# Order of a few decode and output steps in a hybrid attention kernel on one core

## The chip, the cores and the metric

The program runs on one core of a Trainium2 chip. The metric is the device time of one execution in microseconds, and lower is better. All data is fp32 unless a row of the profile says otherwise.

## What is computed

One layer of a model with two kinds of attention, for a prompt of 512 tokens and for 8 decode sequences of one new token each that have 4096 cached tokens. Cut to what matters here:

```python
xn = rmsnorm(x, norm_pre)
(qa, kvc, kvs, kvw, gn, ga, qd, kvd, krp, gb, ma, mb) = split(xn @ w_in)
# branch a (NSA): compressed, selected (top 16 blocks of 64) and window attention, gated and added
o_a = g0 * attend(q, compressed) + g1 * attend(q_rot, selected) + g2 * attend(q_rot, window)
# branch b (MLA): scores over latent pages and their rope rows, softmax, weighted sum of the pages
s = (q_lat @ c.T + q_pe @ kr.T) * MLA_SCALE
o_b = (softmax(s) @ c) @ w_kv_up_v
# merge
pa = (o_a * silu(ga)) @ w_proj_a
pb = (o_b * silu(gb)) @ w_proj_b
h = sigmoid(ma) * pa + sigmoid(mb) * pb
y = x + rmsnorm(h @ w_out, norm_post)
```

It also returns the new cache rows and the shifted window buffer.

## The kernel before

Each engine has its own instruction stream, written out by hand in one function, `build`. Semaphores alone join the streams: `pe.wait_ge(S["dp"], n)` holds TensorE until that semaphore has reached n. The time falls into a projection phase (to about 180 us), the *step loop* (to 456 us), the tail of gates and projections (to 612 us) and the output product with its norm (to the end).

**The step loop** has steps d = 0 to 50. In each step up to 48, the prompt part takes two *units* (a head and a tile of 128 queries). TensorE computes their scores (`scores(d)`, recorded at L1254) for step d, the transposes of the probabilities of step d-1 (`transposes`, L1264), and the output product of step d-2 (`outputs`, L1280). VectorE takes the maxima (L2341), ScalarE the exponentials (L1862), and each copies one of the two transposed units (VectorE L2349, ScalarE by the copy helper L1654). `scores(d)` waits for the exponentials of step d-1.

**Decode work** is dealt out over the same steps by dictionaries that are built by hand. There are 16 *latent pairs* p2 = 0 to 15. Pair p2 reads pages m = 2\*p2 and m = 2\*p2+1 (`latent_scores`, L1362), and with its second page 128 rows of rotary keys, the *rope rows* (L1366). There are also window and selected chunks, whose 512 keys are first transposed (`dec_keys`, L1327, with copies to SBUF by ScalarE and one by VectorE), then scored (`dec_scores`, L1337). `SOFT_at[d]` names the chunk whose softmax falls in step d: latent pairs at 16, 20, 24, 28, 32, 36, 40, 42, 44, 46, 48, others at 17, 22, 25, 26, 29, 30, 33, 34, 37, 38. `K_at` holds the steps with key transposes: 16, 21, 24, 28, 32, 36. `G_at` puts 16 half gates (`gate_half`, L1393, 16 matmuls each) in steps 23 to 49, among them number 14 in step 48 and number 15 in step 49.

The softmax of a chunk goes: scores in bank 5, maximum on VectorE (L2395), exponential on ScalarE into `Pd` (L1879, semaphore `dp`), the *turn* `dec_transposes` on TensorE (L1408), a copy on ScalarE (`dt_copied`; into `PTd` for window and selected chunks), and in the next step the product with the pages (`latent_outputs`, L1377) or the values (`dec_outputs`, L1346), which VectorE folds in (`dec_fold`, L2423 and L2425). The turn stands in one of two places of TensorE's stream: at the end of step d, in bank 7, for the steps in `TURN_FIRST` (17, 20, 22, 25, 26, 29, 30, 33, 34, 37, 38, 40, 42, 44, 46, 48), and otherwise (16, 24, 28, 32, 36) behind `scores(d+1)` in bank 6. The keys use banks 6, 4, 7 and 6 for their four parts, so the turn of a key step waits in bank 6 for ScalarE's copy of the fourth part.

```python
if d - 1 in SOFT_at and d - 1 not in TURN_FIRST:
    dec_transposes(d - 1)
...
if d in TURN_FIRST:
    dec_transposes(d)
```

**Loads.** SyncE issues page loads of 8 x 256 KB each (`latents(m)`, L688), in program order, each behind a wait for its slot. Pages 26 (job `J_LATE`) lie in `W`, over operands of the prompt scores that must be done with. ScalarE issues the rope rows (`load_rope`, L1809), 256 KB a pair, into one buffer, `KRR`: pair p2+1 once the scores of pair p2 are done, and `latent_scores` waits for them ahead of the pair's second page.

**Last rows.** The final product comes in column halves (`out_product`, L1605). VectorE adds each part (`rows_added`, L2739), ScalarE squares it (L1959) and takes the root, VectorE works out the inverse root (`root_of`, L2774 to L2782), and writes y (`out_half`, L2795). For four halves GpSimd multiplies the row by `norm_post` ahead of that; for the last one, (3, 0), it does so in two parts of 256 columns (L875). SyncE stores y.

Of the kernel before, what the change touches and what calls it, by code (L numbers as in the profile page):

```python
# [16 lines left out]
P = 128  # L17
# [146 lines left out]
def build(nc, t):  # L164

    ctx = ExitStack()
    with ctx:
# [157 lines left out]
        for r in range(4):  # L325
# [8 lines left out]
                 J_LATE: [W[:, at:at + 512] for at in (0, 512, 1024, 2048, 8256, 8768, 9280, 9792)]}  # L334
        HALF_PAGES = (cst[:, 1283:1539], OF[:, 1792:2048])

# [80 lines left out]
        TURN_FIRST = {d for d in SOFT_at if d >= 16 and d not in K_at}  # L417
# [200 lines left out]
        def turn_bank(c):  # L618

            return bank[7 if SOFT_STEP[c["q"]] in TURN_FIRST else 6]  # L620

# [4 lines left out]
        def _(sp):  # L626
# [151 lines left out]
            sp.dma_start(t["o_win"][:, 0:WINDOW - 1, :], t["win"][:, 1:WINDOW, :]).then_inc(S["win_moved"], 16)  # L778
# [19 lines left out]
            sp.wait_ge(S["y_out"], 160)  # L798
            sp.wait_ge(S["stored"], QUERIES_MOVED)
            sp.wait_ge(S["win_moved"], 16)  # L800
# [3 lines left out]
        def _(pool):  # L804
# [66 lines left out]
            for part, added in enumerate((out_added["c21a", 1], out_added["c21", 1])):  # L871
                lo = part * 256
                pool.wait_ge(S["z_by_dve"], added)
                pool.wait_ge(S["inv_root"], ROWS_DONE.index(1) + 3)
                pool.tensor_tensor(normed[:, 1536 + lo:1792 + lo], H[:, 3 * D_MODEL + lo:3 * D_MODEL + lo + 256],  # L875
                                   OB[:, lo:lo + 256], ALU.mult).then_inc(S["normed"], 1)

# [54 lines left out]
        def _(pe):  # L932
# [417 lines left out]
            def latent_scores(m):  # L1350
                b, i2, p2 = m // 4, m % 2, m // 2
                if i2 == 1:
                    pe.wait_ge(S["kr_landed"], 16 * (p2 + 1))
                elif mla[p2]["q"]:
                    pe.wait_ge(S["dp"], mla[p2]["q"])
# [8 lines left out]
                if i2 == 1:  # L1364
                    for j in range(4):
                        mm = pe.matmul(bank[5][32 * j:32 * j + 32, 0:P], QRd[:, b * 32:(b + 1) * 32], KRR[:, j * P:(j + 1) * P],  # L1366
# [30 lines left out]
            def dec_transposes(d):  # L1397
# [19 lines left out]
            for d in range(1, PAIRS + 2):  # L1417
# [19 lines left out]
                if d in G_at:  # L1437
# [204 lines left out]
        def _(act):  # L1642
# [1296 lines left out]
```

## Time and profile before

| | us |
|---|---|
| median of 3 runs | 675.36 |
| fastest, slowest of them | 674.79, 683.52 |
| the profiled execution | 675.11 |
| its span on the core | 673.3 |

The rows shown below are of one profiled execution. A timeline row gives start, duration, engine, line, operation, what is written from what is read, the count of merged instructions, and in brackets the idle time of the engine before it with what ended that time. Times are in us from the span's start. "issue" means that the profile shows nothing that the engine waited for.

### The profile page before, as it was taken

The page shows a single profiled execution, that of the slowest core. Times are in us where ns is not written, and L with a number is a line of the kernel's source. Part 1 is how long each engine was busy: PE and PEld are TensorE (multiplying, and loading weights), DVE is VectorE, ACT ScalarE, POOL GpSimd, SP SyncE. Part 2 cuts the span into 40 slices and gives each one's busy share as a digit, 9 for nine tenths or more (in the row PEclk, how much of TensorE's full clock was granted, in tenths as well). Part 3 has the DMA queues.
Part 4 walks back from the last instruction along what each step waited for, and adds up shares of the span by engine and source line. Part 5 has one row for each costly group of instructions (what it writes and reads, how often), then busy time and mean ns, then how long its engine had stood idle before and what let it go on. Part 6 is the DMA issues. An engine that isn't in the chain of part 4 may idle for free.

```text
span 673.3 us, 15352 instructions
## 1 busy us (share of the span) xinstructions
PE 651.5 (97%) x5771; PEld 433.0 (64%) x5771; DVE 447.4 (66%) x1232; ACT 214.8 (32%) x586; POOL 79.5 (12%) x91
## 2 busy tenths in 40 slices
PE   9999999999999998899999998999999999999994
PEld 3444444553576765667777675678788888886442
DVE  2198899686577777766665663637585757649864
ACT  0311321776444454444443532421011111110221
POOL 0344343125000000120211000000000000000011
PEclk9999999999999999999999999999999999999997
DMA  8999999999989999978759789975411111027011
GB/s 337 417 422 424 424 427 400 361 369 283 344 296 378 398 395 413 374 245 316 273 179 361 230 276 403 407 280 219 157 63 63 63 63 63 1 109 300 2 63 62
DMA packets 67587, 179.44 MB, mean 267 GB/s; under 512 B 7513, under 2 KB 16498, under 8 KB 60218
## 3 DMA queue, kind: packets, MB, share of 16 engines
q1 hardware_dynamic: 56088, 125.14, 50.9%
q0 software_dynamic: 8640, 48.90, 17.9%
q10 hardware_dynamic: 2786, 4.42, 1.8%
q8 instruction: 46, 0.75, 0.4%
q14 instruction: 27, 0.22, 0.1%
HBM read 169.38 MB, written 12.72 MB: 270 GB/s over the span
## 4 chain that ended last, share of the span: by engine, by line
PE 88%; DVE 5%; issue 2%; ACT 2%; SPq 1%; DMA 1%; DVEq 0%; another core or an unknown queue 0%; ACTq 0%
PE bank L1554 20%; PE bank L973 12%; PE bank L1393 8%; PE bank L1605 7%; PE bank L1254 5%; PE bank L958 4%; PE bank L1377 4%; PE bank L1362 3%; PE bank L1280 3%; PE bank L1264 3%; PE bank L1583 2%; PE bank L1137 2%; PE bank L1327 2%; PE bank L1337 1%; PE bank L1408 1%
## 5 line engine op out<-in xcount | busy, mean ns | idle before, releaser
L973 PE MATMUL bank<-W,XG 128*128 128x494 f32 x192 | 83.5, 579 | 0.0
L1862 ACT ACTIVATE projP<-bank,projP 128x128 f32<-128x128 f32 (+3 forms) x96 | 49.8, 523 | 41.8 <-DVE projP L2341 41.5
L2641 DVE TENSOR_TENSOR projP<-projP,bank 128x260 f32<-128x260 f32 x81 | 32.6, 423 | 42.3 <-PE bank L1554 41.6
L1654 ACT ACTIVATE projP<-bank 128x128 f32<-128x128 f32 (+5 forms) x87 | 33.7, 391 | 84.0 <-PE bank L1554 47.7
L1393 PE MATMUL bank<-W 128*128 128x260 f32 x256 | 60.4, 389 | 0.0
L973 PEld LDWEIGHTS bank<-W,XG 128*128 128x128 f32 x192 | 35.2, 192 | 35.6 <-issue 35.0
L1393 PEld LDWEIGHTS bank<-W 128*128 128x128 f32 x256 | 47.3, 190 | 10.8 <-issue 3.7
L2341 DVE CUSTOM_DVE_ANT_0 bank<-bank,maskb 128x128 f32<-128x128 f32 (+3 forms) x96 | 45.8, 511 | 12.0 <-PE bank L1254 10.6
L1654 ACT ACTIVATE W<-bank 128x512 f32<-128x512 f32 (+2 forms) x69 | 40.1, 582 | 38.7 <-PE bank L1016 11.6
L809 POOL DMA_INDIRECT ring<-cmp,idxi x32 | 38.6, 1207 | 67.5 <-DVE VV L2052 47.7
L1254 PE MATMUL bank<-W 64*128 64x128 f32 (+7 forms) x192 | 46.0, 466 | 0.5 <-ACT projP L1862 0.4
L2052 DVE TENSOR_TENSOR VV<-ring 128x1024 f32<-128x1024 f32 x32 | 39.2, 1223 | 7.4 <-DMA ring<-cmp,idxi 5.1
L869 POOL TENSOR_TENSOR ring<-XG,OB 128x512 f32<-128x512 f32 x3 | 3.8, 1264 | 303.5 <-DVE XG L2739 303.5
L1554 PE MATMUL bank<-ring 128*128 128x260 f32 x168 | 38.2, 383 | 0.0
L1264 PE MATMUL bank<-cst,projP 128*128 128x128 f32 x240 | 36.7, 280 | 0.3
L1554 PEld LDWEIGHTS bank<-ring 128*128 128x128 f32 x168 | 31.8, 190 | 5.3 <-issue 0.4
L1554 PE MATMUL bank<-W 128*128 128x260 f32 x144 | 34.6, 383 | 0.0
L1939 ACT ACTIVATE projP<-projP 128x260 f32<-128x260 f32 x28 | 11.3, 420 | 71.0 <-DVE projP L2641 70.9
L1264 PEld LDWEIGHTS bank<-cst,projP 128*128 128x128 f32 x240 | 26.8, 140 | 9.6 <-issue 5.3
L1986 DVE TENSOR_SCALAR projP<-projP,sm 128x128 f32<-128x128 f32 (+3 forms) x64 | 28.7, 448 | 2.3
L1554 PEld LDWEIGHTS bank<-W 128*128 128x128 f32 x144 | 27.2, 190 | 4.1
L1605 PE MATMUL bank<-ring,W 128*128 128x512 f32 x64 | 28.3, 592 | 0.0
(477 smaller groups left out, 1165.7 us busy)
## 6 DMA issues: line engine op xcount, KB each, us to landing
ring<-latent SPq DMA_DIRECT2D x168, 256.0 KB
XG<-latent SPq DMA_DIRECT2D x56, 256.0 KB
W<-w_gate SPq DMA_DIRECT2D x12, 1024.0 KB, 4.7
W<-w_attn SPq DMA_DIRECT2D x16, 494.0 KB, 11.7
W<-latent SPq DMA_DIRECT2D x20, 256.0 KB, 4.9
rope_rows<-ring SPq DMA_DIRECT2D x16, 256.0 KB, 7.0
KRR<-rope_rows ACTq DMA_DIRECT2D x16, 256.0 KB
ring<-win SPq DMA_DIRECT2D x8, 512.0 KB
```

Of the source, the lines that this page charges most:

```text
L809: pool.indirect_dma_start(out=dst, out_offset=None, in_=src, in_offset=bass.IndirectOffsetOnAxis(ap=rows, axis=0)).then_inc(sem, 16)
L973: mm = pe.matmul(bank[2 * (u % 2) + n][:, 0:GW], XG[:, k * TOK + tl * P:k * TOK + (tl + 1) * P], w_part(half, k, n), start=(k == 0), stop= ...
L1254: pe.matmul(bank[x % 2][:, 0:width], q, kk, start=True, stop=True).then_inc(S["s"], 1)
L1264: mm = pe.transpose(pt_bank(u)[:, kb * P:(kb + 1) * P], Pb[u % 4][:, kb * P:(kb + 1) * P], ident)
L1393: mm = pe.matmul(bank[6][:, 0:HALF], gate_w[g % 2][:, at:at + P], X2[:, k * TOK + hf * HALF:k * TOK + (hf + 1) * HALF], start=(k == 0), st ...
L1554: mm = pe.matmul(pair_bank(v, name)[:, 0:HALF], stationary(a, kk), moving(b, kk), start=(kk == 0), stop=(kk == inner - 1))
L1605: mm = pe.matmul(bk[:, lo:hi], lhs, rhs, start=(kk == 0), stop=(kk == 3))
L1654: return act.activation(dst, src, ACT.Copy, scale=scale)
L1862: act.activation(Pb[u % 4][:, 0:w], bank[u % 2][:, 0:w], ACT.Exp, bias=NMp[:, u:u + 1], scale=-1.0, accum_out=RSp[:, u:u + 1]).then_inc(S[ ...
L2052: dve.tensor_tensor(sum4, x[:, 0:1024], x[:, 1024:2048], ALU.add).then_inc(S["summed"], 1)
L2341: dve.tensor_tensor_reduce(bank[u % 2][:, 0:w], bank[u % 2][:, 0:w], maskb[:, 512 - w:512], -1.0, 1e38, ALU.add, ALU.min, NMp[:, u:u + 1]) ...
L2641: dve.tensor_tensor(out, a, pair_bank(v, product)[:, 0:HALF], ALU.add).then_inc(S["z_by_dve"], 1)
```

## The change

- The turn of every softmax from step 16 on uses bank 7 (`TURN_IN_7`). The turns of steps 17, 20, 22, 42 and 44 move from the end of their step to behind the next step's scores.
- The rope rows of pairs 13 and 15 get a place of their own, `PTd`. Pair 13 is then loaded in step 40 beside pair 12, pair 14 in step 42, and pair 15 in step 44.
- Half of the pages of m = 26 are loaded ahead of m = 22 to 24. The other half no longer waits for the scores of step 39. Two of its places in `W` change.
- In step 48 the half gate 14 comes behind the last transposes and the turn. Its tanh and silu move to step 49.
- The last row's product with `norm_post` moves from GpSimd to VectorE, in two parts. The add of the last 256 columns comes ahead of `out_half(1, 0)`.
- The store of the window buffer counts on the semaphore `y_out` (no effect on the order).

```diff
+        ROPE_APART = (13, 15)
+        def rope_home(p2):
+            return PTd[:, :] if p2 in ROPE_APART else KRR[:, 0:512]
+        def rope_landed(eng, p2):
+            if p2 in ROPE_APART:
+                eng.wait_ge(S["rope_apart"], 16 * (ROPE_APART.index(p2) + 1))
+            else:
+                eng.wait_ge(S["kr_landed"], 16 * sum(1 for x in range(p2 + 1) if x not in ROPE_APART))
...
-        TURN_FIRST = {d for d in SOFT_at if d >= 16 and d not in K_at}
+        TURN_IN_7 = {d for d in SOFT_at if d >= 16}
+        TURN_FIRST = {d for d in TURN_IN_7 if d not in K_at and d not in (17, 20, 22, 42, 44)}
...
             gate(3)
+            sp.wait_ge(S["s"], 64)
+            latents(26, 0, 4)
             for m in range(22, 25):
                 latents(m)
             sp.wait_ge(S["ds"], max(c["q"] for c in chunks if c["kind"] == "slc") + 1)
-            sp.wait_ge(S["s"], 80)
-            latents(26)
+            latents(26, 4, 8)
             latents(25)
...
-                    pe.wait_ge(S["keys_by_A"], 3 * keys_before(d + 1) - (d in K_at and d in TURN_FIRST))
-                if d in TURN_FIRST:
+                    pe.wait_ge(S["keys_by_A"], 3 * keys_before(d + 1) - (d in K_at and d in TURN_IN_7))
+                if d in TURN_IN_7:
                     pe.wait_ge(S["do"], c["q"])
...
-                if d in G_at:
+                if d in G_at and d != PAIRS:
                     gate_half(d)
...
                 if d in TURN_FIRST:
                     dec_transposes(d)
+                if d == PAIRS:
+                    gate_half(d)
...
             def load_rope(p2):
-                if p2:
-                    act.wait_ge(S["ds"], mla[p2 - 1]["q"] + 1)
+                if p2 == ROPE_APART[0]:
+                    act.wait_ge(S["do_ps"], sum(1 for c in chunks if c["kind"] != "mla"))
+                elif p2:
+                    act.wait_ge(S["ds"], mla[p2 - 2 if p2 > ROPE_APART[0] else p2 - 1]["q"] + 1)
...
+                if d == PAIRS + 1:
+                    gate_silu(G_at[PAIRS])
...
             root_of(1, 1)
+            dve.wait_ge(S["z_by_dve"], out_added["c21a", 1])
+            last_normed(0)
             dve.wait_ge(S["sqz"], SQUARES.index((3, 0, "a")) + 1)
             dve.tensor_tensor(vfirst[:, 3:4], vfirst[:, 3:4], ssz[:, 10:11], ALU.add).then_inc(S["mean_sq"], 1)
+            rows_added("c21", 1, rows(3, 0), rows(3, 0), "p4", 256, 512)
             out_half(1, 0)
-            rows_added("c21", 1, rows(3, 0), rows(3, 0), "p4", 256, 512)
+            dve.wait_ge(S["z_by_dve"], out_added["c21", 1])
+            last_normed(256)
             out_half(1, 1)
             root_of(3, 0)
```

## Rows read from the trace of the kernel before

**Rows 1.** The page's first part: busy time, share of the span, instructions.

```profile
PE 651.5 (97%) x5771; PEld 433.0 (64%) x5771; DVE 447.4 (66%) x1232; ACT 214.8 (32%) x586; POOL 79.5 (12%) x91
```

**Rows 2.** TensorE's waits over the span: us in total, times, longest us.

```profile
PE bank L1280 <- DVE projP L2349: 2.7, 5, 0.8
PE bank L1408 <- ACT W L1879: 1.9, 4, 0.8
PE bank L1377 <- issue: 1.4, 1, 1.4
PE bank L1408 <- ACT W L1654: 1.4, 3, 0.6
```

**Rows 3.** Timeline at the turn of step 16, a key step.

```profile
248.74 0.60 ACT L1654 ACTIVATE W<-bank 128x512 f32<-128x512 f32 x1 [0.84 <-PE bank L1327]
249.48 0.30 PE L1408 MATMUL bank<-cst,W 128*128 128x128 f32 x1 [0.36 <-ACT W L1654]
249.71 1.06 PE L1337 MATMUL bank<-W 128*32 128x512 f32 x8
```

**Rows 4.** Timeline at the turn of step 17, to the scores of step 20.

```profile
254.07 0.63 PE L1408 MATMUL bank<-cst,W 128*128 128x128 f32 x4 [0.33 <-DVE projP L2425]
254.63 0.70 PE L1254 MATMUL bank<-W 64*128 64x256 f32 x4
...
255.89 0.47 ACT L1862 ACTIVATE projP<-bank,projP 128x256 f32<-128x256 f32 x1 [0.56 <-DVE projP L2341]
...
260.30 0.92 PE L1254 MATMUL bank<-W 64*128 64x384 f32 x4 [0.43 <-ACT projP L1862]
```

**Rows 5.** Timeline at the turn of step 22 and behind it.

```profile
276.32 0.66 PE L1408 MATMUL bank<-cst,W 128*128 128x128 f32 x4 [0.81 <-ACT W L1879]
...
277.69 0.55 DVE L2349 COPY projP<-bank 128x384 f32<-128x384 f32 x1
...
278.86 0.84 PE L1280 MATMUL bank<-projP,VV 128*32 128x128 f32 x24
```

**Rows 6.** Stretches: us, busy of PE, PEld, DVE, ACT, POOL, clock, DMA share, GB/s.

```profile
373.00:378.00 5.00, 4.91 (x67) 2.51 (x66) 3.64 (x14) 3.33 (x10) 0.00 (x0) 1.00 0.05 16
...
391.00:394.00 3.00, 3.00 (x94) 2.27 (x91) 2.40 (x7) 1.73 (x5) 0.00 (x0) 1.00 0.17 33
...
394.00:408.00 14.00, 13.32 (x215) 10.26 (x213) 7.99 (x36) 4.07 (x16) 0.00 (x0) 1.00 0.99 348
```

**Rows 7.** SyncE's loads of pages 26, then 25, 27 and 28.

```profile
392.54 4.83 SPq L688 DMA_DIRECT2D W<-latent  x8
398.12 14.82 SPq L688 DMA_DIRECT2D ring<-latent  x24
```

**Rows 8.** Timeline of steps 42 to 44.

```profile
408.15 1.08 PE L1362 MATMUL bank<-ring,projP 128*32 128x128 f32 x32 [0.83 <-DMA ring<-latent]
...
409.33 0.20 ACT L1862 ACTIVATION_READ_ACCUMULATOR projP<-bank,projP 128x1 f32 x1
...
410.34 0.33 PE L1408 MATMUL bank<-cst,W 128*128 128x128 f32 x1 [0.31 <-ACT W L1879]
...
411.23 1.08 PE L1362 MATMUL bank<-W,projP 128*32 128x128 f32 x32
...
423.66 0.33 PE L1408 MATMUL bank<-cst,W 128*128 128x128 f32 x1 [0.53 <-ACT W L1879]
```

**Rows 9.** Timeline of step 49.

```profile
449.41 1.08 PE L1280 MATMUL bank<-projP,VV 128*32 128x128 f32 x32 [0.68 <-DVE projP L2349]
```

**Rows 10.** Timeline of the last rows, VectorE.

```profile
662.69 0.42 DVE L2739 TENSOR_TENSOR XG<-XG,bank 128x256 f32<-128x256 f32 x1 [0.97 <-PE bank L1605]
...
663.90 1.22 DVE L2795 SCALAR_TENSOR_TENSOR XG<-XG,sm,ring 128x512 f32<-128x512 f32 x1
...
665.04 0.41 DVE L2739 TENSOR_TENSOR XG<-XG,bank 128x256 f32<-128x256 f32 x1
...
667.27 0.75 DVE L2795 SCALAR_TENSOR_TENSOR XG<-ring,sm 128x512 f32<-128x512 f32 x1
```

More of the change, by code:

```diff
@@ L333, in build @@
                  + [OF[:, 768 + i * 512:1280 + i * 512] for i in range(2)] + [None],
-                 J_LATE: [W[:, at:at + 512] for at in (0, 512, 1024, 2048, 8256, 8768, 9280, 9792)]}
+                 J_LATE: [W[:, at:at + 512] for at in (0, 512, 2048, 3072, 8256, 8768, 9280, 9792)]}
         HALF_PAGES = (cst[:, 1283:1539], OF[:, 1792:2048])
+        ROPE_APART = (13, 15)
[6 more added lines that the diff above has]
+                eng.wait_ge(S["kr_landed"], 16 * sum(1 for x in range(p2 + 1) if x not in ROPE_APART))
         def slot_of(n):
@@ L618, in turn_bank @@
         def turn_bank(c):
-            return bank[7 if SOFT_STEP[c["q"]] in TURN_FIRST else 6]
+            return bank[7 if SOFT_STEP[c["q"]] in TURN_IN_7 else 6]
         block = ctx.enter_context(nc.Block())
@@ L777, in _ @@
             gate(5)
-            sp.dma_start(t["o_win"][:, 0:WINDOW - 1, :], t["win"][:, 1:WINDOW, :]).then_inc(S["win_moved"], 16)
+            sp.dma_start(t["o_win"][:, 0:WINDOW - 1, :], t["win"][:, 1:WINDOW, :]).then_inc(S["y_out"], 16)
             for g in range(6, 12):
@@ L870, in _ @@
                                    OB[:, hf * 512:(hf + 1) * 512], ALU.mult).then_inc(S["normed"], 1)
[L871 to L876, printed above, removed]
         GROUPS = [(C_Q + P * k, P) for k in range(4)] + [(C_KS, P), (C_KW, P)] + [(C_Q + P * k, P) for k in range(4)] \
@@ L1352, in latent_scores @@
                 if i2 == 1:
-                    pe.wait_ge(S["kr_landed"], 16 * (p2 + 1))
+                    rope_landed(pe, p2)
                 elif mla[p2]["q"]:
@@ L1365, in latent_scores @@
                     for j in range(4):
-                        mm = pe.matmul(bank[5][32 * j:32 * j + 32, 0:P], QRd[:, b * 32:(b + 1) * 32], KRR[:, j * P:(j + 1) * P],
+                        mm = pe.matmul(bank[5][32 * j:32 * j + 32, 0:P], QRd[:, b * 32:(b + 1) * 32], rope_home(p2)[:, j * P:(j + 1) * P],
                                        start=False, stop=True)
@@ L1808, in load_rope @@
                     act.wait_ge(S["rope_out1"], 128)
-                act.dma_start(KRR[:, 0:512], rope_rows[p2 * P:(p2 + 1) * P]).then_inc(S["kr_landed"], 16)
+                act.dma_start(rope_home(p2), rope_rows[p2 * P:(p2 + 1) * P]).then_inc(S["rope_apart" if p2 in ROPE_APART else "kr_landed"], 16)
             group_copied(act, 15)
@@ L1916, in _ @@
                     dec_exp(c)
-                    if c["kind"] == "mla" and c["no"] < 15:
-                        load_rope(c["no"] + 1)
-                if d in G_at:
+                    if c["kind"] == "mla" and c["no"] < 14:
+                        load_rope(c["no"] + (1 if c["no"] < 12 else 2))
+                    if c["kind"] == "mla" and c["no"] == 11:
+                        load_rope(13)
+                if d == PAIRS + 1:
+                    gate_tanh(G_at[PAIRS])
+                if d in G_at and d != PAIRS:
                     gate_tanh(G_at[d])
@@ L2459, in _ @@
                     pt_copy(2 * (d - 2))
+                if d == PAIRS + 1:
+                    gate_silu(G_at[PAIRS])
                 if d < PAIRS:
@@ L2478, in _ @@
                     read_out(d - 2)
-                if d in G_at:
+                if d in G_at and d != PAIRS:
                     gate_silu(G_at[d])
@@ L2791, in out_half @@
                     pos = LAST_HALVES.index((x, half))
-                    dve.wait_ge(S["normed"], 5 if x == 3 else pos + 1)
+                    if x < 3:
+                        dve.wait_ge(S["normed"], pos + 1)
                     src = normed[:, pos * 512:(pos + 1) * 512]
```

5 lines of the change are left out of this document (3 added, 2 removed).

## The prediction

> **What bounds the kernel now.** I read the page's first part, then the list of waits, then the timeline around each place that the diff touches. TensorE is busy 651.5 of 673.3 us [rows 1], so in all it can give back 21.8 us, and much of that lies outside the change: before the loop, and behind the last product. The waits of TensorE inside the step loop are short and named one by one: transposed units that VectorE has not copied yet (2.7 us in 5 places), turns that wait for the exponential of their chunk (1.9 us in 4), turns that wait for the fourth key copy (1.4 us in 3), one stop of 1.4 us that nothing explains [rows 2], and one page that lands late (0.83 us) [rows 8]. All these lines are the loop's; the list has no wait of TensorE of this size in the tail, so what the loop gives back arrives at the end undiminished. The sum is therefore a list of gaps of some tenths, each of which has to be asked: what is late next?
>
> **The change, part by part.**
>
> **Turns of the five key steps (16, 24, 28, 32, 36), bank 7 in place of 6.** In step 16 the fourth key copy starts on ScalarE at 248.74 and takes 0.60, the turn waits 0.36 us for it and starts at 249.48, and the decode scores start at 249.71 [rows 3]. In bank 7 the turn needs the copy of the third part alone and can fill the wait. But the decode scores behind it read the fourth part too, so they can start at 249.48 at the earliest: the gain is not the wait of 0.36 but the place that the turn took, 249.71 less 249.48, 0.23 us. There are three such waits, 1.4 us together [rows 2]: 3 x 0.23 = 0.7. The other two key steps have no wait of that kind in the list. The bounds are 0 and 0.23 each; I take 0.1 each, for a gap too short to be listed. Together 0.9, bounds 0 and 1.15. No new wait comes in: bank 7 must be folded first, which the key transposes of the same step already demand.
>
> **Turn of 17 behind the scores of 18.** The turn waits 0.33 us for VectorE's fold [rows 4]. The scores need no fold and can start at 254.07 - 0.33 = 253.74. They take 0.70, so the turn starts at 254.44, 0.37 later than before, and ends 0.63 later, at 255.07. ScalarE's copy of it (0.60, the length of the same copy form in [rows 3]) ends at 255.67, and behind it on ScalarE stand the exponentials of step 18, which started at 255.89: 0.2 earlier. From them hangs the chain by VectorE and ScalarE for which the scores of step 20 wait 0.43 us [rows 4]. Gain 0.2; at worst the later copy holds the decode product, a loss of 0.37; at best the 0.33.
>
> **Turn of 20 behind the scores of 21.** The next thing for which TensorE waits is VectorE's copy in step 21, the longest of its kind, 0.8 us [rows 2]. VectorE does not wait for the turn, so the gain goes into that wait: 0, bounds 0 and 0.3.
>
> **Turn of 22 behind the scores of 23.** The wait is 0.81 us, and the scores fill it. Late next is VectorE's copy, from 277.69 for 0.55, to 278.24; the outputs that need it started at 278.86 [rows 5]. Gain 278.86 - 278.24 = 0.6, bounds 0 and 0.8.
>
> **Pages 25 and 26, and the turn of 42.** SyncE issued pages 26 from 392.54 and pages 25 from 398.12 [rows 7], after a stretch in which the DMA moved 33 GB/s; then it ran full, at 348 GB/s [rows 6]. Two pages are 4.2 MB, that is 12 us at this rate, from 394 to 406 and some latency: the page that TensorE waited 0.83 us for, until 408.15 [rows 8]. After the change half of 26 has gone long before, and the other half waits for nothing of step 39, so it fills the hole from 391 to 394 or lands before it. Pages 25 wait for their slot until the decode output of step 39 is done, at most 3 us behind the scores of step 39 that released pages 26 at 392.54: by 395.5. Then they have only themselves and two rope loads in the queue, 2.6 MB or 7.5 us: 403. The need is at 408.15 - 0.83 = 407.3, some 4 us later, and the wait goes. The turn of 42 waits another 0.31 us for its exponential [rows 8]. They don't add up in full: the scores of step 43 need the exponentials of step 42, which end at 409.33 + 0.20 = 409.53 and hang on VectorE, not on the page. Then 0.70 for the scores [rows 4] and 0.33 for the turn give 410.56, where the next pages' products started at 411.23 [rows 8]: gain 0.7, bounds 0.3 and 1.1.
>
> **Turn of 44 behind the scores of 45.** The wait is 0.53 us [rows 8]; the exponentials of the prompt stand ahead of the chunk's own on ScalarE, so the scores are free to start. Gain 0.5, bounds 0 and 0.5.
>
> **Gate 14 behind the turn of 48.** In step 49 the outputs wait 0.68 us for VectorE's copy of the last transposes [rows 9], because these came last before them. Now the 16 gate matmuls, several us, stand between, and cover the copy. Gate 15 must wait for the silu of 14, moved to step 49; the outputs (1.08 us [rows 9]) and latent products lie between them, which is more than a tanh and a silu of one 260-column tile should take (an add of 256 columns takes 0.42 [rows 10]). Gain 0.7, bounds 0 and 0.7.
>
> **Rope rows.** No wait of TensorE in the list is for `KRR`, and none is long enough to hide one [rows 2]. The parts of their own gain nothing and cost nothing that TensorE sees: each is 0.26 MB, 0.75 us of the DMA at 348 GB/s [rows 6], under the 4 us that pages 25 have to spare. With that cover gone it would cost 0.75.
>
> **Half of 26 early.** It puts 1 MB, 3 us at the same rate, ahead of pages 22 to 24. They are first read in step 39, and from 373 to 378 the DMA moved 16 GB/s [rows 6]: that hole takes it in. Nothing; with no hole, up to 3 us later pages, of which I expect none to be waited for. The new wait for 64 scores was met in step 31, and SyncE stands later than that.
>
> **Last rows.** VectorE gets two products of 128x256; the nearest row is the add of that size, 0.42, so +0.8 if nothing comes back. Two things do: `out_half(1, 0)` took 1.22 where its like takes 0.75, 0.5 back, and the add of the last columns no longer stands behind it at 665.04 [rows 10]. It could start about when its product ends, at some 664.4 (an estimate: the first part's add at 662.69, and half of the last 16 matmuls). Bounds -0.6 (the earlier add carries through) and +0.8; I take 0. Why 1.22: GpSimd's product ran beside it. The Trainium skill (GPSIMD Engine Reference, Specifications) says that GpSimd's SBUF interfaces are shared with VectorE and contend with instructions that have two SBUF inputs, as this one has. By that rule the 0.5 comes back and the end stays; without it the end would be 0.4 to 0.5 later, which stays within my range.
>
> **The sum.** 0.9 + 0.2 + 0 + 0.6 + 0.7 + 0.5 + 0.7 + 0 = 3.6 us. The profiled execution took 675.11 (span 673.3, 1.8 around it), so 671.5; it stands 0.25 under the median of 675.36, so the median becomes 675.36 - 3.6 = 671.8, and the span 669.7.
>
> **The rivals.**
>
> *The gains are taken back by VectorE and ScalarE.* Each moved turn comes later than before, and so does its copy. TensorE waited longest in total for VectorE [rows 2]. If 22, 44 and 48 lose all of their gain and 17 costs 0.3, then 3.6 - 0.6 - 0.5 - 0.7 - 0.5 = 1.3: 674.1. Against it: in 22 I have already counted VectorE's copy.
>
> *The unexplained stop goes too.* The 1.4 us [rows 2] lies in step 43, between two products of which all that the second needs had been there; the DMA was full, and the change takes 1 MB out of that stretch. Without it: 3.6 + 1.4 = 5.0, 670.4. For it speaks only the coincidence.
>
> *More such stops: slower.* If these stops are TensorE's instruction fetch behind page loads, each new one costs 1.4 us, and the place is where the change adds traffic, around 361 to 364 and from 386 on. Two of them leave 0.8 us of the gain; three give 3.6 - 4.2 = -0.6, 676.0: it decides from three on. Against it: one stop of this size in the long full stretches of the loop. The Trainium skill (Runtime: NRT & Kernel Launch, Instruction fetch mechanics) holds that the fetch is prefetched in order and hidden by the issue rate. By that rule there would be none of these stops, neither one more nor the one that stands, and the time would be the sum's; the row of 1.4 us neither shows a fetch nor excludes one.
>
> *It does nothing* (the waits only change their names): 675.4. The decode scores of the key steps and gate 14 speak against, since there a wait is filled with work that has to be done anyway.
>
> **How the numbers follow.** The sum holds, within 1 us: 0.50. Taken back by the other engines: 0.22. The stop goes: 0.12. Three or more new stops: 0.07. Nothing: 0.09. The likeliest gives 671.8. The range reaches from 669.8, below the case without the stop, to 675.0, over the case of gains taken back; it leaves out the two last cases and the far low end, under 0.2. All cases lie within 2% (13.5 us, about what a measurement of this kernel can tell from no change): the bounds of all terms together give at most 5.5 us, and the stop 1.4 more. So faster by over 2% 0.01, within 2% 0.98, slower 0.01.
>
> **What would show it.** In the changed kernel's waits of TensorE: no turn waits for ScalarE's key copy, and the key scores (L1337's successor) wait for it instead, with 0.1 to 0.3 us each; no wait for a page in step 42; turns no longer wait for their exponential in 22, 42 and 44; the wait of 0.68 us in step 49 gone, and none ahead of gate 15. SyncE issues pages 25 by 395.5 where it was 398.12 [rows 7]. The last VectorE row ends as far behind the last matmul as before. The first product of the tail comes some 3.6 us earlier. I am wrong if the loop ends there but the total does not follow, or if new waits for VectorE's copies of over 1.5 us together appear.

## The result, and the profile after

| | before | after |
|---|---|---|
| median, us | 675.08 (4 runs) | 666.42 (4 runs) |
| fastest, slowest | 673.16, 683.52 | 665.78, 666.93 |
| profiled execution, its span | 675.11, 673.3 | 665.78, 664.0 |

The ratio is 0.9863, with a 95% interval of 0.9823 to 0.9903. The forecast was 671.8 with a range of 669.8 to 675.0: the direction was right and "within 2%" too, but the change saved 9.3 us between the two profiled executions and 8.7 between the medians, where the sum said 3.6, and the time lies below the range. The 683.52 is one execution 1.5% above the fastest of its kernel, and nothing below rests on it.

TensorE's waits in the changed kernel from 200 to 470 us (us in total, times, longest) answer to [rows 2], whose rows are those of this stretch too:

```profile
PE bank L1285 <- DVE projP L2362: 2.3, 4, 1.0
PE bank L1259 <- ACT projP L1871: 0.9, 3, 0.4
PE bank L1351 <- issue: 0.4, 1, 0.4
```

Gone are all waits of the turn (before: for L1879, L1654 and L2425), the one for a page, and both stops of over 1 us with "issue". The list of before had two of these. [rows 2] shows the one of 1.4 us, and the forecast speaks of "one stop of 1.4 us that nothing explains"; the other stood right behind the last row shown:

```profile
PE bank L1337 <- issue: 1.1, 1, 1.1
```

New is the 0.4 us of L1351, the decode product of step 18 (see the turn of 17 below). Line numbers have shifted: L1254 is now L1259, L1280 is L1285, L1362 is L1367, L1377 is L1382, L1408 is L1413, L1605 is L1612, L2739 is L2754, L2795 is L2811.

Where the time went, read off at the start of `scores(d)` and at two later places. The second column of gains starts from another execution of the unchanged kernel (`b_again`), which matters below:

| place | before | after | gain | gain against b_again |
|---|---|---|---|---|
| scores(16) | 243.42 | 243.46 | 0.0 | -0.2 |
| scores(22) | 270.71 | 270.07 | 0.6 | 0.4 |
| scores(23) | 276.90 | 273.82 | 3.1 | 1.9 |
| scores(24) | 285.08 | 282.95 | 2.1 | 1.0 |
| scores(42) | 406.62 | 403.33 | 3.3 | 2.1 |
| scores(44) | 419.96 | 414.29 | 5.7 | 5.8 |
| scores(46) | 432.30 | 426.09 | 6.2 | 6.3 |
| first product of the tail | 455.76 | 448.76 | 7.0 | 7.1 |
| last matmul | 664.00 | 657.00 | 7.0 | 7.1 |
| end of the span | 673.3 | 664.0 | 9.3 | 9.4 |

So 7.0 us come from the loop and arrive undiminished at the last matmul, as forecast; 2.3 more come behind the last matmul, where the sum had 0.

**Steps 42 and 43 of the changed kernel**, TensorE (start, duration, engine, line, operation, tiles, count, idle time before):

```profile
403.33 0.70 PE L1259 MATMUL bank<-W 64*128 64x256 f32 x4
403.96 1.08 PE L1367 MATMUL bank<-ring,projP 128*32 128x128 f32 x32
...
406.30 0.70 PE L1259 MATMUL bank<-W 64*128 64x256 f32 x4 [0.45 <-ACT projP L1871]
406.93 0.33 PE L1413 MATMUL bank<-cst,W 128*128 128x128 f32 x1
407.19 1.08 PE L1367 MATMUL bank<-W,projP 128*32 128x128 f32 x32
408.08 0.40 PE L1285 MATMUL bank<-projP,VV 128*32 128x128 f32 x8
408.30 1.05 PE L1382 MATMUL bank<-XG,projP 128*32 128x256 f32 x16
```

The page is there when TensorE comes (before: 0.83 us late, [rows 8]), the scores of step 43 wait 0.45 us for their exponentials, which the forecast had named as the next bound, and the products of L1382 follow without the stop. In the kernel before, these products began so:

```profile
413.96 1.07 PE L1377 MATMUL bank<-XG,projP 128*32 128x256 f32 x16 [1.43 <-issue]
```

**The end of the program.** L167 is the end of the block in which all engines' streams lie; each stream ends there with a DRAIN, and one semaphore event on all engines closes the program. Of its rows in the kernel before (duration ns min/median/max; first and last start):

```profile
L167 POOLq DRAIN  x1: 7585/7585/7585, 665.5 to 665.5; - x1
L167 SPq DRAIN  x1: 7/7/7, 671.0 to 671.0; - x1
L167 PEldq EVENT_SEMAPHORE  x1: 51/51/51, 673.3 to 673.3; - x1
```

and in the changed kernel:

```profile
L167 POOLq DRAIN  x1: 7688/7688/7688, 654.8 to 654.8; - x1
L167 SPq DRAIN  x1: 7/7/7, 663.8 to 663.8; - x1
L167 PEldq EVENT_SEMAPHORE  x1: 51/51/51, 663.9 to 663.9; - x1
```

Before, SyncE had waited for its last store by 671.0, and the program ended at 673.3: when GpSimd's drain was over, 665.5 + 7.6 = 673.1. After, GpSimd's drain is over at 654.8 + 7.7 = 662.5, ahead of the stores (663.8), and the program ends with the stores.

### The profile page after: what moved, and what is told of

It reads as the page before. It is cut to its first block, busy times and chain, and to the rows that moved or that the text cites. A ratio compares the mean times of both kernels' runs of the same rounds, so it can differ in the third digit from the quotient of the medians.

```text
span 664.0 us, 15351 instructions
## 1 busy us (share of the span) xinstructions
PE 651.1 (98%) x5771; PEld 433.6 (65%) x5771; DVE 446.4 (67%) x1234; ACT 214.7 (32%) x586; POOL 77.7 (12%) x89
## 4 chain that ended last, share of the span: by engine, by line
PE 92%; DVE 5%; issue 1%; ACT 1%; DVEq 0%; ACTq 0%
PE bank L1561 20%; PE bank L978 12%; PE bank L1398 9%; PE bank L1612 7%; PE bank L1259 5%; PE bank L1382 4%; PE bank L963 4%; PE bank L1285 4%; PE bank L1367 4%; PE bank L1269 4%; PE bank L1590 2%; PE bank L1142 2%; PE bank L1332 1%; PE bank L1342 1%; PE bank L1220 1%
## 5 line engine op out<-in xcount | busy, mean ns | idle before, releaser
L1259 PE MATMUL bank<-W 64*128 64x128 f32 (+7 forms) x192 | 46.0, 466 | 0.9 <-ACT projP L1871 0.9
L1612 PE MATMUL bank<-ring,W 128*128 128x512 f32 x64 | 28.3, 592 | 0.0
```

Of the source, the lines that this page charges most:

```text
L1259: pe.matmul(bank[x % 2][:, 0:width], q, kk, start=True, stop=True).then_inc(S["s"], 1)
L1612: mm = pe.matmul(bk[:, lo:hi], lhs, rhs, start=(kk == 0), stop=(kk == 3))
```

## The experiments

Each was timed beside the kernel before on the same chip. All but `f_nopages`, `f_nolast`, `x_late`, `v_scale` and `a_again` start from the kernel before; these five start from the changed one.

Nothing that the change touches lies ahead of `scores(16)`, and yet the profiled executions reach it at times up to 1.2 us apart (243.21 in `e_pages`, 244.44 in `a_again`, and 251.27 in `f_nolast`, see there). So the loop is best compared by lengths:

| kernel | `scores(16)` to `scores(44)` | `scores(44)` to the tail's first product | last matmul to the end |
|---|---|---|---|
| before | 176.54 | 35.80 | 9.3 |
| b_again | 176.86 | 35.79 | 9.3 |
| e_rope | 176.57 | 35.79 | 9.3 |
| e_last | 175.75 | 35.79 | 7.0 |
| e_gate | 175.81 | 35.01 | 9.3 |
| e_turns | 173.84 | 35.27 | 9.3 |
| e_pages | 173.42 | 35.80 | 9.3 |
| f_nopages | 174.91 | 34.46 | 7.0 |
| after, a_again | 170.83 | 34.47 | 7.0 |

The first five have turns and page order of before up to `scores(44)`; their spread of 1.1 us is what one profiled execution of such a part leaves open.

### Two executions of what is not changed

`b_again`, no edit.

> The kernel before, unchanged, profiled a second time. Theory A (the two stops that no semaphore explains, 1.4 us before a latent product in step 43 and about 1 us before the key scores of step 22, are late instruction fetches that differ from run to run): at least one of them is missing or has another size here, and the span lies 0 to 2.5 us under 673.3. Theory B (they belong to this program's order): both stand again within 0.2 us, and the span is 673.3 within 0.3. The ratio to the kernel before is 1.000 either way.

675.39 us, ratio 1.0002 [0.9992, 1.0012]. The sum of its time agrees, but not its course, and neither theory is right as a whole: one stop is missing and the other has another size, and yet the span is the same (673.4). In the profile of before, TensorE stood 1.14 us in step 22, behind a fourth key copy that began at 272.29; the second execution has neither:

```profile
271.56 1.07 PE L1337 MATMUL bank<-W 128*32 128x512 f32 x8
...
408.17 1.93 PE L1362 MATMUL bank<-ring,projP 128*32 128x128 f32 x32 [2.02 <-DMA ring<-latent]
...
414.07 1.07 PE L1377 MATMUL bank<-XG,projP 128*32 128x256 f32 x16 [0.39 <-issue]
```

Its scores of step 42 start at 405.44, 1.2 us earlier than in the profile of before, and the page lands at the same time as there (408.17 against 408.15). So it waits 2.02 us and not 0.83. Behind that wait its matmuls run for 3.5 us at a granted clock of 0.51 (the 1.2 GHz level):

```profile
408.20:411.70 3.50, 3.50 (x51) 2.77 (x51) 1.04 (x5) 0.71 (x5) 0.00 (x0) 0.51 1.05 405
```

(a stretch, busy of PE, PEld, DVE, ACT, POOL, clock, DMA share, GB/s). That in turn shortens the stop of L1377 to 0.39, and the product goes on at 414.07 against 413.96. So between these two executions 1.2 us gained ahead of the page were lost by then, to the page, the clock and the stop together. That is not a law of the place: `e_last` comes to `scores(42)` 0.8 us earlier than before (405.85) and passes the stop 0.8 us earlier (413.18), and `e_turns` keeps its gain too.

### The parts alone

`e_turns`, all turns in bank 7 and 17, 20, 22, 42, 44 moved, nothing else:

```diff
-        TURN_FIRST = {d for d in SOFT_at if d >= 16 and d not in K_at}
+        TURN_IN_7 = {d for d in SOFT_at if d >= 16}
+        TURN_FIRST = {d for d in TURN_IN_7 if d not in K_at and d not in (17, 20, 22, 42, 44)}
```

> Only the turns: bank 7 for all from step 16 on, and those of 17, 20, 22, 42 and 44 behind the next scores. By my sum: 0.9 + 0.2 + 0 + 0.6 + 0.3 + 0.5 = 2.5 us less. Rival A (the stop of 1.4 us in step 43 and that near step 22 go with the turns): 4.5 to 5 us less. Rival B (the stops belong to the page traffic): both still there, 2.5 us less or under.

672.98 us, 0.997 [0.9953, 0.9988], 2.1 us under the median of before in the same run. In the profile it is 2.8 us ahead of `b_again` at the tail's first product, though it reached `scores(16)` 0.8 us later. Between `scores(16)` and `scores(42)` it gains 2.3 on `b_again`, and keeps it: its page 25 is issued (395.75) and lands earlier too. Of the two rivals B holds for step 43 (the stop of step 22 is missing here as in every other execution). The wait and the stop are still there:

```profile
405.85 1.08 PE L1363 MATMUL bank<-ring,projP 128*32 128x128 f32 x32 [1.26 <-DMA ring<-latent]
...
411.84 1.07 PE L1378 MATMUL bank<-XG,projP 128*32 128x256 f32 x16 [1.98 <-issue]
```

The stop has grown to 1.98 us, from 1.43 in before and 0.39 in `b_again`: from the page's products to the start of the stop it is 4.0 us (405.85 to 409.86) where it was 4.4 (408.15 to 412.53), because the turn of 42 no longer waits, and the stop takes that back.

`e_pages`, only the order of pages 25 and 26 and two places in `W`:

```diff
             gate(3)
+            sp.wait_ge(S["s"], 64)
+            latents(26, 0, 4)
             for m in range(22, 25):
                 latents(m)
             sp.wait_ge(S["ds"], max(c["q"] for c in chunks if c["kind"] == "slc") + 1)
-            sp.wait_ge(S["s"], 80)
-            latents(26)
+            latents(26, 4, 8)
```

> Only the order of the page loads (half of pages 26 early, the other half not held for step 39, two places in W). By my sum: the wait for the page in step 42 goes, 0.8 us, of which 0.3 comes back at the turn of 42: 0.5 us less. Rival (the unexplained stop of 1.4 us in step 43 is TensorE's instruction fetch behind page loads): it goes too, 1.9 to 2.2 us less. If the stop stays, the rival falls for this traffic.

672.84 us, 0.9975 [0.996, 0.9989], 2.3 us under the median of before in the same run, nearer to the rival's 1.9 to 2.2 than to the sum's 0.5; in the profile 3.4 us less than `b_again` at the tail. Both the page wait and the stop are gone, and the turn of 42 waits longer for its exponential (0.80, where it was 0.31):

```profile
405.96 1.08 PE L1363 MATMUL bank<-ring,projP 128*32 128x128 f32 x32
...
408.64 0.33 PE L1409 MATMUL bank<-cst,W 128*128 128x128 f32 x1 [0.80 <-ACT W L1880]
...
410.65 1.05 PE L1378 MATMUL bank<-XG,projP 128*32 128x256 f32 x16
```

`f_nopages`, the changed kernel with the old page order:

> The changed kernel with the order of its page loads undone (pages 26 whole, behind the scores of step 39, at their old places); turns, rope rows, gate 14 and last rows as changed. Theory (the late page and the late fetch are both the page order's, 0.8 to 2.0 and 1.4 to 2.0 us): both come back in steps 42 and 43, and the time is 2.5 to 3.5 us above the changed kernel, near 669.5. Rival (with the turns moved the waits overlap and the page order is worth only what my sum gave, 0.7): 667.1.

669.50 us, 0.9905 [0.9888, 0.9921], about 3 us above the changed kernel, as expected. Wait and stop are back, 1.49 and 1.98 us:

```profile
406.87 1.08 PE L1367 MATMUL bank<-ring,projP 128*32 128x128 f32 x32 [1.49 <-DMA ring<-latent]
...
412.86 1.07 PE L1382 MATMUL bank<-XG,projP 128*32 128x256 f32 x16 [1.98 <-issue]
```

`e_gate`, only half gate 14 behind the turn of 48 (`if d in G_at and d != PAIRS` at the old place, `if d == PAIRS: gate_half(d)` behind the turn, its tanh and silu in step 49):

> Only gate 14 behind the turn of 48. My sum: the wait of 0.68 us for VectorE's copy in step 49 goes, nothing else changes: between the scores of step 47 and the first product of the tail 0.7 to 0.8 us less than in the kernel before. Rival (the wait moves to gate 15 behind the silu of 14): the same distance as before.

674.09 us in its one run (median of before beside it: 675.53); one run decides nothing, so the length in the profile has to. The wait of 0.68 [rows 9] is gone, and no other took its place:

```profile
444.79 3.67 PE L1393 MATMUL bank<-W 128*128 128x260 f32 x16
448.39 1.08 PE L1280 MATMUL bank<-projP,VV 128*32 128x128 f32 x32
```

From `scores(44)` to the tail it gains 0.8 on `b_again`.

`e_rope`, only the rope rows in places of their own (with the window store counted on `y_out`, as in the change):

> Only the rope rows of pairs 13 and 15 in a place of their own, with the order of their loads. My sum: nothing; the waits of TensorE in steps 42 to 48 stay as in the kernel before, ratio 1.000. Rival (the extra 0.26 MB beside pages 25 costs what it takes at full rate): the page of step 42 is waited for 0.7 us longer.

675.53 us, 1.000 [0.9989, 1.0012], and 0.05 us at the tail: nothing, as forecast. Its page wait in step 42 is 1.92 us, no more than the 2.02 of the unchanged kernel in `b_again`.

The loop's parts add up in the profiles. From `scores(16)` to the tail's first product it is 212.34 us in before, 209.11 with the turns alone and 209.22 with the pages alone; 3.2 and 3.1 less, and 0.8 for the gate (from `scores(44)` on), are 7.1, where the whole gives 7.0 (205.30). Against `b_again` (212.65) the parts give 7.7 and the whole 7.35.

### What the stop of L1377 is

What comes late together with the stop is a packet of the queue named "instruction". The DMA view of before from 411.6 to 411.8 shows one among 42 packets of pages (count, MB, share of 16 engines' time in the window):

```profile
q1 hardware_dynamic: 42, 0.08, 100.9%
q8 instruction: 1, 0.02, 29.2%
```

It is the 33rd packet of 16 KB that this queue moves; there are 46 in a run. TensorE makes this stop always at the same instruction, the first L1377 of step 43:

| kernel | 33rd packet starts | first L1377 of step 43 | stop with "issue" |
|---|---|---|---|
| before | 411.64 | 413.96 | 1.43 |
| b_again | 411.72 | 414.07 | 0.39 |
| e_turns | 409.38 | 411.84 | 1.98 |
| f_nopages | 410.40 | 412.86 | 1.98 |
| e_rope | 411.76 | 414.02 | 1.43 |
| e_gate | 411.38 | 413.72 | 1.43 |
| e_last | 410.89 | 413.18 | 1.43 |
| e_pages | 405.96 | 410.65 | none |
| after | 404.58 | 408.30 | none |
| a_again | 405.38 | 409.29 | none |
| x_late | 406.40 | 409.53 | none |
| v_scale | 405.54 | 409.12 | none |
| f_nolast | 412.12 | 416.13 | none |

Where there is a stop, it ends 2.3 to 2.5 us behind the packet's start; these are the seven executions of kernels with the old order of the page loads. Where the packet came over 3 us ahead, there is none. The test was to bring the packet forward without a change to where pages lie: `x_hold` keeps SyncE from issuing pages 27 to 29 until the scores of step 42 are done.

```diff
             latents(26)
             latents(25)
+            sp.wait_ge(S["ds"], next(c["q"] for c in chunks if c["kind"] == "mla" and c["no"] == 12) + 1)
             for m in range(27, 30):
                 latents(m)
```

> The kernel before, but SyncE holds the loads of pages 27 to 29 until the scores of step 42 are done (some 409 us), so that behind pages 26 and 25 nothing stands in the queues. Fetch theory (the stop of 1.4 us ahead of the latent product in step 43 is TensorE waiting for its next 16 KB of instructions, whose packet started at 411.6, held up by page loads, and each time 2.3 us before TensorE went on): the packet starts by 408, and the stop is gone, while the wait for page 25 in step 42 stays near 0.8 us. Rival (the stop follows from the late page itself): page wait and stop both stay. Later pages may now be late themselves, so the whole time is not the test: up to 2 us either way.

The packet starts at 405.45, and L1378 of step 43 has no stop, with the page order of before. The page of step 42 is still late, by 1.65 us, so the stop does not follow from the late page:

```profile
409.30 1.08 PE L1363 MATMUL bank<-ring,projP 128*32 128x128 f32 x32 [1.65 <-DMA ring<-latent]
...
412.39 1.08 PE L1363 MATMUL bank<-W,projP 128*32 128x128 f32 x32
413.28 0.40 PE L1281 MATMUL bank<-projP,VV 128*32 128x128 f32 x8
413.50 1.05 PE L1378 MATMUL bank<-XG,projP 128*32 128x256 f32 x16
```

Two of the expected figures were missed: this page wait, for which 0.8 was expected, and the whole time. The price is later pages in the steps behind, and the kernel is 5.1 us slower where 2 at most were expected, 680.61 us, 1.0073 [1.0053, 1.0093]:

```profile
PE bank L1363 <- DMA ring<-latent: 7.4, 5, 2.5
```

So the stop comes and goes with the packet, by two different edits. That the packet brings TensorE's own code is inferred; the trace does not name the packet's content. Three things speak for it: the one instruction at which TensorE stops, the nearly constant delay, and a count. In the order of time, the stop is ahead of the 8642nd instruction of TensorE's stream in the trace (matmuls, weight loads and waits). `f_nopages` and `v_scale` (see below) have a second, smaller stop ahead of the 8386th, exactly 256 instructions earlier, and it goes with the packet before, the 32nd:

| kernel | 32nd packet starts, takes | stop ends | stop with "issue" |
|---|---|---|---|
| f_nopages | 397.87, 0.88 | 400.19 | 0.24 |
| v_scale | 396.04, 2.14 | 399.67 | 0.16 |

Behind the packet's end that is 1.4 and 1.5 us, and the seven stops of step 43 end 1.3 to 1.5 us behind the end of the 33rd, which takes 0.93 or 0.94.

### The end of the program

`e_last`, only the last rows:

```diff
-            for part, added in enumerate((out_added["c21a", 1], out_added["c21", 1])):
-                lo = part * 256
-                pool.wait_ge(S["z_by_dve"], added)
...
             root_of(1, 1)
+            dve.wait_ge(S["z_by_dve"], out_added["c21a", 1])
+            last_normed(0)
...
+            rows_added("c21", 1, rows(3, 0), rows(3, 0), "p4", 256, 512)
             out_half(1, 0)
-            rows_added("c21", 1, rows(3, 0), rows(3, 0), "p4", 256, 512)
+            last_normed(256)
```

> Only the last rows of the change: GpSimd's last two products move to VectorE. Theory A (the program can't end before GpSimd has drained, which took 7.6 us from the start of its last product in the profile of before): GpSimd's last product now starts some 3.7 us earlier, its drain ends before the stores do, and the program ends about 2.1 us earlier than before; the last VectorE row stays within 0.2 us of its distance to the last matmul. Theory B (the 2.1 us came from elsewhere, the stores or the window store's semaphore): the end stays within 0.3 us of before.

672.59 us, where before had 675.11 in the same run; the interval of the ratio, 0.9987 [0.995, 1.0024], is too wide to decide. In its profile the end comes 7.0 us behind the last matmul, where before has 9.3. `f_nolast` and `a_again`, timed side by side, decide: the changed kernel with the last rows undone, and the changed kernel itself.

> The changed kernel with the last rows alone undone (GpSimd multiplies the last row again, order of the adds as before). If the end hangs on the drain of GpSimd, the end comes 9.26 us behind the last matmul where it was 6.93, and the time is 2.3 us above that of the changed kernel in the same run: 668.7. If the prediction's term of 0 was right and the difference came with the chip or the loop, it is equal within 0.3 us. The loop is untouched: the first product of the tail at 448.8 as in the changed kernel, within 0.9 (the one-off stop).

> The changed kernel unchanged, to compare with: 666.4, first product of the tail at 448.8, end 6.93 behind the last matmul; neither a page wait nor an issue stop of over 0.5 us in steps 42 and 43, the 33rd large instruction packet by 406.

`f_nolast` took 669.12 us (0.9915 [0.9898, 0.9931]) and `a_again` 666.81 us (0.9886 [0.9867, 0.9905]): 2.3 us. The profiled execution of `f_nolast` came some 7 us late out of the projection phase, where its granted clock was 0.97 in place of 1.00, unlike its other five runs; its loop and its end are to be read by differences. From `scores(16)` to the tail it took 205.3 us, as the changed kernel did. The end lies 674.1 - 664.83 = 9.3 us behind the last matmul, and again it is GpSimd's drain, 666.3 + 7.6 = 673.9, that is over last:

```profile
L167 POOLq DRAIN  x1: 7583/7583/7583, 666.3 to 666.3; - x1
L167 SPq DRAIN  x1: 7/7/7, 671.7 to 671.7; - x1
```

In `a_again` the end is 7.0 us behind the last matmul. Is it GpSimd's last instruction that counts, or the work that VectorE took over? `x_late` is the changed kernel with one more instruction on GpSimd, which nobody reads:

```diff
+            pool.wait_ge(S["y"], 8)
+            pool.memset(late[:, :], 0.0)
```

> The changed kernel with one GpSimd memset of 128x1 added, held until the eighth half row of y is written (about 659.5 us), on which nothing depends. Drain theory (the end waits for GpSimd's drain, 6.4 us past its last instruction): the last VectorE row and the stores stay, the end comes at about 659.5 + 0.1 + 6.5 = 666.1 to 667, 2 to 3 us later than the changed kernel. Rival (the drain is only as long because it waits for the others, and always ends with the stores): no change, 0.2 us at most.

```profile
660.79 0.10 POOL L885 MEMSET late<- 128x1 f32 x1 [3.49 <-DVE XG L2814]
...
L167 POOLq DRAIN  x1: 6480/6480/6480, 660.8 to 660.8; - x1
L167 SPq DRAIN  x1: 7/7/7, 665.0 to 665.0; - x1
```

669.21 us, 0.9901 [0.9884, 0.9917]: 0.10 us of work that nothing waits for makes the program end 2.4 us behind its stores (665.0, 667.4), and 9.25 us behind its last matmul in place of 7.0. The rival, that this drain always ends with the stores, falls. The drain ends 6.4 us behind the end of GpSimd's last instruction here (660.89 to 667.3) and in before (665.53 + 1.17 = 666.70 to 673.1).

### An attempt at more

The largest wait left in the changed kernel is 1.0 us in step 21, for VectorE's copy, behind three scalings of 128x260 (L2452). `v_scale` deals these out as 2, 2, 2, 2, 3, 3, 2 over steps 19 to 25 in place of 3 a step from 20:

> The changed kernel with VectorE's 16 input scalings dealt out over steps 19 to 25 as 2, 2, 2, 2, 3, 3, 2 in place of three a step from 20 on. Theory (TensorE's longest wait left, 1.0 us for VectorE's copy in step 21, stands behind the three scalings of step 20, 0.43 us each): with two there the copy comes 0.4 us earlier, and again in steps 22 and 23; 0.4 to 0.8 us less than the changed kernel. Rival (the scalings of step 19 delay the maxima there, for which the exponentials and the scores of step 20 wait): no gain or 0.5 us more.

666.76 us, 0.9883 [0.9866, 0.9899]: no gain on the changed kernel, as the rival said. The copy is now waited for less, and an exponential more; up to `scores(41)` the loop is 0.1 us longer than in the changed kernel, and 0.8 more go in step 41, where the small stop at the 8386th instruction stands:

```profile
263.41 0.92 PE L1259 MATMUL bank<-W 64*128 64x384 f32 x4 [0.57 <-ACT projP L1871]
...
265.28 0.65 PE L1285 MATMUL bank<-projP,VV 128*32 128x128 f32 x16 [0.70 <-DVE projP L2362]
```

## Why the prediction was wrong, and where it was right

**"I take 0" for the last rows: wrong by 2.3 us, the largest single miss.** The working behind it was right as far as it went. VectorE's last row starts 657.00 to 660.79, 3.8 us behind the last matmul, where it was 664.00 to 667.94, 3.9; and `out_half(1, 0)` took 0.75 in place of 1.22 [rows 10]:

```profile
657.42 0.42 DVE L2754 TENSOR_TENSOR XG<-XG,bank 128x256 f32<-128x256 f32 x1 [0.18 <-PE bank L1612]
657.76 0.75 DVE L2811 SCALAR_TENSOR_TENSOR XG<-XG,sm,ring 128x512 f32<-128x512 f32 x1
...
660.79 0.74 DVE L2811 SCALAR_TENSOR_TENSOR XG<-XG,sm,ring 128x512 f32<-128x512 f32 x1
```

The 0.5 us came back as the row of 1.22 beside GpSimd's product had suggested, and in `f_nolast`, with GpSimd's product back, the row takes 1.22 again. By this the trace agrees with the rule of the Trainium skill (GPSIMD Engine Reference, Specifications) on the shared SBUF interfaces; no number stands there to compare. Which of the two engines pays is not fixed: before, VectorE's next row of this kind took 0.74 while GpSimd's second product, which began inside it, took 1.17 in place of 0.72.

What failed was the unspoken step from VectorE's last row to the end of the program. The sum took the end to follow VectorE and the stores, but in the kernel before nothing of them was last. The span ended 673.3 - (667.94 + 0.75) = 4.6 us behind VectorE, and the rows of the program's end, which the forecast did not read, name GpSimd: its last product, one of the two that the change moves, ended at 666.70, and the drain was over 6.4 later. The change takes the last work off the engine whose drain closes the program, and nothing in the sum priced that. The gain is bounded by the stores: after, the program ends 0.2 behind SyncE's DRAIN, and by that the kernel before would have ended at 671.2, which is 2.1 of the 2.3; the rest is VectorE's.

**"gain 0.7, bounds 0.3 and 1.1" for the pages and the turn of 42: wrong by 1.7 us.** The page's wait and the turn's wait went as the forecast worked them out, and the scores of step 43 did become late for their exponential. From `scores(42)` to the next pages' products it is 3.86 us (403.33 to 407.19) in place of 4.61 (406.62 to 411.23): 0.75, where 0.7 was counted. SyncE was even earlier than the 395.5 expected:

```profile
383.60 1.98 SPq L700 DMA_DIRECT2D W<-latent  x4
390.77 17.73 SPq L700 DMA_DIRECT2D ring<-latent  x24
```

The failed step is to have kept the unexplained stop of 1.4 us apart, as a rival with a chance of 0.12, for which spoke "only the coincidence". `e_pages` shows that the same page order makes both the late page and the stop, and `x_hold` that the stop hangs on the pages that stand in the queue, and not on the late page. The gain from `scores(42)` to `scores(44)` is 5.7 - 3.3 = 2.4 against before: 0.75, the stop of 1.43, and 0.2 that no run here explains. Against `b_again` it is even 3.7, since there the page was waited for 2.0 us. The other rival, "three or more new stops", took the same mechanism with the opposite sign: no new stop of this kind came, since the change relieves the queue there. Against it the forecast held that there was "one stop of this size"; the row of 1.1 us, which it passed over, is not shown to be of this kind. The Trainium skill (Runtime: NRT & Kernel Launch, Instruction fetch mechanics) has the fetch hidden behind the issue rate. If the packet is TensorE's code, these runs do not agree with it: in seven executions TensorE stands 0.4 to 2.0 us and goes on 2.3 to 2.5 us behind a packet's start.

**The turns of the key steps: 1.4 us and not 0.9.** The mechanism was right: the turn fills ScalarE's copy, and the decode scores wait for that copy instead. The term was short because it took the old start of the turn as the earliest start of the scores. Step 24, before, ScalarE's fourth key copy and what follows it:

```profile
291.50 0.60 ACT L1654 ACTIVATE W<-bank 128x512 f32<-128x512 f32 x1 [0.84 <-PE bank L1327]
...
292.35 0.30 PE L1408 MATMUL bank<-cst,W 128*128 128x128 f32 x1 [0.47 <-ACT W L1654]
292.58 1.06 PE L1337 MATMUL bank<-W,projP 128*32 128x512 f32 x8
```

and after:

```profile
289.37 0.60 ACT L1661 ACTIVATE W<-bank 128x512 f32<-128x512 f32 x1 [0.84 <-PE bank L1332]
289.69 0.33 PE L1413 MATMUL bank<-cst,W 128*128 128x128 f32 x1
290.07 1.07 PE L1342 MATMUL bank<-W,projP 128*32 128x512 f32 x8
```

Before, the turn started 0.25 us behind the end of the copy (292.10); after, the decode scores start 0.10 behind it (289.97). From the scores of step 25 to the decode scores it is 0.81 (289.26 to 290.07) in place of 1.19 (291.39 to 292.58): 0.38 gained. The three steps with a wait gave 0.28 (16), 0.38 (24) and 0.47 (32), where 0.23 each was counted; the other two gave 0.13 each, where 0.1 was counted. The sign named for it, waits of 0.1 to 0.3 us, did not show: the decode scores wait 0.05 us in the three steps, too short to be listed.

**The turn of 17: 0.4 and not 0.2.** Steps 16 to 20 gave 0.68, of which 0.28 is step 16. The bound was 0.33, so this term, too, was a little outside. The path was right, its sum too slow: it laid the durations end to end. In the changed kernel the turn started 0.63 us behind the start of the scores (253.44, 254.07), where 0.70 was counted, and the exponentials started 0.11 ahead of the recorded end of ScalarE's copy of the turn, 254.77 + 0.60 = 255.37:

```profile
254.77 0.60 ACT L1661 ACTIVATE W<-bank 128x512 f32<-128x512 f32 x1 [0.94 <-PE bank L1413]
...
255.26 0.47 ACT L1871 ACTIVATE projP<-bank,projP 128x256 f32<-128x256 f32 x1
...
255.46 1.08 PE L1351 MATMUL bank<-ring,W 128*32 128x128 f32 x32 [0.38 <-issue]
```

The later copy did hold the decode product, as the forecast feared at worst. The last row is the stop of L1351 in the list above; the profile names no releaser, but it ends 0.09 us behind the copy that the product reads, and it stands in all seven executions with the moved turns. It cost nothing, since the scores of step 20 hang on the exponentials.

**Right within 0.1:** the turn of 20 (0, the wait went into VectorE's copy, now 1.0 us), the turn of 22 (0.5, forecast 0.6), the turn of 44 (0.5, forecast 0.5), gate 14 (0.8, forecast 0.7), the rope rows (0), the early half of pages 26 (0, no wait for pages 22 to 24 came), and that the loop's gain arrives at the end.

**A stop that was in the profile by chance.** The stop of step 22 (1.1 us, L1337 with "issue") was in none of the other executions, of before or of a kernel with one part, so some 1.0 us (0.95 between `scores(22)` and `scores(24)`) of the 3.3 gained up to `scores(42)` against the profile of before is not the change's. It cost nothing in the whole, since the page wait behind it was shorter by 1.2. In the profile of before ScalarE's fourth key copy began late (272.29) and the stop ends 0.1 us behind the copy's end; why the copy was late, no run here shows. Why the page landed within 0.3 us of the same time in four executions (408.15, 408.17, 408.21, 407.91; a fifth, `e_last`, had 407.37), whether TensorE came at 407.3 or at 406.1, is not settled: SyncE issued it in `b_again` 0.6 us earlier (397.50 against 398.12), and it landed no earlier.

In all: 0.5 (key steps) + 0.2 (turn 17) + 1.7 (pages and stop) + 2.3 (end) + 1.0 (the stop of step 22) are the 5.7 us between 3.6 and 9.3; the small terms (0.1 and -0.1) cancel.

## What to carry to other kernels

Read the last rows of every engine, not of the busiest one alone: work that nobody waits for can set the end if its engine closes last. Here, taking it off GpSimd was worth the time by which GpSimd's drain ended behind the stores. A stop with "issue" inside a stretch where the DMA is full is to be priced together with the page loads around it, since an edit that takes loads out of the queue there can remove both; and a wait that such an edit leaves in place can grow by what was gained just ahead of it, as the stop of step 43 did in `e_turns`. One profile shows one execution: a second one of the unchanged kernel tells which waits are the kernel's.

## What the runs showed of the hardware that was not expected

- GpSimd's drain at the end of the program ended 6.4 us behind the end of its last instruction, with a product of 1.17 us (before), a product of 1.27 us (after, 656.07 to 662.5) and a memset of 0.10 us (`x_late`) alike. VectorE's drain ended 0.1 us behind its last row (before, 668.69 to 668.8).
- TensorE stopped for 0.4 to 2.0 us at one fixed instruction in the seven executions in which a packet of 16 KB of the instruction queue, among page loads, started late: it went on 2.3 to 2.5 us behind the packet's start, 1.3 to 1.5 behind its end. In the seven others the packet started 3.1 to 8 us ahead of that instruction, and there was no stop there.
- After a wait of 2.02 us in `b_again` the granted clock was 0.51 for 3.5 us; after 1.92 us in `e_rope`, at the same instruction, and after the stop of 1.98 us in `e_turns`, it stayed at 1.00.
- A row of VectorE with two inputs in SBUF (128x512) took 1.22 us beside a product on GpSimd and 0.75 alone; the two GpSimd products of the same size (128x256) took 0.72 beside the row of 1.22, and 1.17 beside one of 0.74.
